# Moving two products of a gated linear recurrence from VectorE to GpSimd, and its decay constant into ScalarE's scale operand

## The chip, the core and the metric

The kernel runs on one core of one Trainium2 chip. A core has engines with queues of their own, each of which works strictly in order: TensorE (PE in the profile; its weight loads are PEld), VectorE (DVE), ScalarE (ACT), GpSimd (POOL) and SyncE (SP), which only issues transfers here. They wait for each other through semaphores. The metric is the device time of one execution in microseconds (us), lower is better; the times given are medians of several runs.

## The reference

The computation is three transformer-like layers for one sequence of 256 tokens with a width of 2048: a block of sparse attention and a mixture of 32 experts, an "even" layer and an "odd" layer. The change touches only the even layer. Its first half is a gated linear recurrence with 1024 channels in 8 blocks of 128:

```python
def rg_lru(x, gx_w, gx_b, ga_w, ga_b, lru_lambda):
    B, S, _ = x.shape
    xb = x.reshape(B, S, LRU_BLOCKS, LRU_BLOCK_DIM)
    gate_i = jax.nn.sigmoid(jnp.einsum("bsnd,nde->bsne", xb, gx_w) + gx_b).reshape(B, S, LRU_WIDTH)
    gate_r = jax.nn.sigmoid(jnp.einsum("bsnd,nde->bsne", xb, ga_w) + ga_b).reshape(B, S, LRU_WIDTH)
    log_a = -LRU_C * jax.nn.softplus(-lru_lambda.astype(jnp.float32)) * gate_r.astype(jnp.float32)
    a = jnp.exp(log_a)
    mult = jnp.sqrt(-jnp.expm1(2.0 * log_a))
    u = mult * gate_i.astype(jnp.float32) * x.astype(jnp.float32)
...
    _, h = lax.associative_scan(combine, (a, u), axis=1)
    return h.astype(x.dtype)
...
    y_a = rg_lru(lru_x, gx_w, gx_b, ga_w, ga_b, lru_lambda) * jax.nn.silu(lru_gate)
```

The second half is sliding-window attention. Both halves are joined and multiplied by the output weights `w_out`.

## The kernel before

Everything is stored with channels on the 128 partitions and the 256 tokens along the free axis. A projection is done in single chunks of 128 output channels. Its weights arrive as two halves of 128x1024; ScalarE rounds each half to a high part (`hi`, L1636), VectorE subtracts to get the low part (`lo`, L1945), and TensorE multiplies high by high, low by high and high by low (L1185): 24 matmuls of 128x256 for a half, 48 for a chunk. Four halves are kept in split form, so ScalarE and VectorE split a half while TensorE uses an earlier one.

The order of the work is written out by hand. `order_bc` makes one list of steps for each engine, and each engine runs its list from top to bottom, waiting before a step for the named steps of other engines. The stretch that matters here is the loop over the 24 chunks `bs`, `lx`, `lg` (window gate, recurrence input, recurrence gate; 8 of each). It mixes three kinds of work:

- The projections themselves. ScalarE moves a result out of PSUM (L1588 for `lx`, L1590 for `lg`), and GpSimd multiplies it by the row norm (`rms`, L2421, 128x256). Those products are all that GpSimd does in this stretch.
- Attention jobs, one after every second chunk. VectorE prepares the softmax (`soft`: L1865 mask, L1868 maximum, L1872 to L1874 small sums), ScalarE takes the exponentials (`exp`, L1722, L1724), VectorE divides (`scale`: L1882, L1883, L1898), TensorE transposes (`T`, L1119), ScalarE copies (`pt`, L1733), TensorE multiplies with the values (`O`, L1127), VectorE multiplies with the gate (`out`, L1911).
- The recurrence, in four pairs of blocks, started after chunks `lx 3`, `lx 6`, `lg 1` and `lg 4` (pairs 0 to 3). TensorE computes both gates (`lgate`, L1401); ScalarE takes sigmoids (L1600, L1601); VectorE multiplies the input gate by the input and the decay gate by its constant (`lruA`, L2294, L2295); ScalarE takes the exponential and the tangent of both blocks at once (`lruB`, L1747, L1748); VectorE combines them (`lruC`, L2300, L2301); ScalarE takes a root (`lruD`, L1751); VectorE multiplies and scans (`lruE`, L2307, L2308). `lruB` and `lruC` follow one chunk after the gates, `lruD` and `lruE` two chunks after.

After `lg 3` ScalarE applies silu to the first four gate chunks (L1684) and VectorE multiplies them with the first four blocks of the recurrence (`lmul 0`, L2312, 128x1024); `lmul 1` does the rest after `lg 7`. The result is then split for the output projection `wb` (L1671 and L1964).

The gates of the odd block of a pair go to one of the two PSUM banks of the projections. So the next but one projection that needs this bank waits for the sigmoids (L1601).

Of the kernel before, what the change touches and what calls it, by code (L numbers as in the profile page):

```python
# [19 lines left out]
ALU = mybir.AluOpType  # L20
# [23 lines left out]
LRU_C = 8.0  # L44
# [548 lines left out]
def order_bc():  # L593
# [53 lines left out]
    def lru_gates(p):  # L647
        for n in (2 * p, 2 * p + 1):
            o.add("pe", "lgate", n)
            if n % 2:  # L650
                o.acc.append(("lgate", n))
            o.add("act", "evac", ("lgate", n))
            o.add("dve", "lruA", n)
# [10 lines left out]
    for k, x in enumerate(rest):  # L664
# [12 lines left out]
        if x == ("lg", 3):  # L677
            o.add("act", "silu", "lg", 0, 4)
            o.add("dve", "lmul", 0)
# [119 lines left out]
def program(nc, t):  # L799
    with ExitStack() as ctx:  # L800
# [111 lines left out]
        cL, tsp = small[:, 144:152], small[:, 152:192]  # L912
# [586 lines left out]
        def _(act):  # L1499
# [8 lines left out]
            def run(k, o):  # L1508
# [5 lines left out]
                def needs(engine, *step):  # L1514
                    act.wait_ge(done[k][engine], o.at[engine][step])
# [99 lines left out]
                for step in o.steps["act"]:  # L1615
# [44 lines left out]
                    elif what == "mh":  # L1660
# [8 lines left out]
                        if made_by:  # L1669
                            needs("dve", *made_by)  # L1670
# [73 lines left out]
                    elif what == "lruB":  # L1744
                        p = step[1]
                        needs("dve", "lruA", 2 * p + 1)
                        act.activation(W(bLA, 2), W(bGR, 2), ACT.Exp, scale=-1.0)  # L1747
                        ins = act.activation(W(bTH, 2), W(bGR, 2), ACT.Tanh)  # L1748
# [50 lines left out]
        def _(dve):  # L1799
# [32 lines left out]
            def run(k, o):  # L1832
# [6 lines left out]
                def needs(engine, *step):  # L1839
                    dve.wait_ge(done[k][engine], o.at[engine][step])  # L1840
# [81 lines left out]
                for step in o.steps["dve"]:  # L1922
# [330 lines left out]
                    elif what == "softplus2":  # L2253
# [15 lines left out]
                        prod = W(aQI)[:, 0, 0:128].rearrange("p (a d) -> p a d", a=2)  # L2269
                        dve.tensor_scalar(cL, cL, LRU_C, None, ALU.mult)  # L2270
# [19 lines left out]
                    elif what == "lruA":  # L2290
                        n = step[1]
                        needs("act", "evac", ("lgate", n))
                        g = W(bGR + n % 2)[:, 0, :]
                        dve.tensor_tensor(W(bGI + n % 2)[:, 0, :], W(bGI + n % 2)[:, 0, :], W(bY + n)[:, 0, :], ALU.mult)  # L2294
                        ins = dve.tensor_scalar(g, g, cL[:, n:n + 1], None, ALU.mult)  # L2295
# [6 lines left out]
                    elif what == "lruE":  # L2302

                        n = step[1]
                        needs("act", "lruD", n // 2)
                        gi, th, a = (W(z + n % 2)[:, 0, :] for z in (bGI, bTH, bLA))
# [95 lines left out]
        def _(pool):  # L2402
# [3 lines left out]
            for count, (what, x) in enumerate(BC.steps["pool"]):  # L2406
                if count:
                    pool.wait_ge(done[1]["pool"], count)
                if what == "lo":
# [4 lines left out]
                                             WHs[1][:, x % PARTS, 0:n].bitcast(F32), ALU.subtract)  # L2414
                elif what == "rms":
# [122 lines left out]
```

## Time and profile before

| | us |
|---|---|
| median of 3 runs | 2349.46 |
| lowest, highest | 2347.33, 2351.78 |
| the profiled execution's own time | 2358.7 |
| its span, first to last instruction | 2356.9 |

| engine | busy us | share of the span |
|---|---|---|
| PE | 2089.4 | 89% |
| DVE | 1252.0 | 53% |
| ACT | 858.9 | 36% |
| POOL | 55.2 | 2% |

The shares are means over stages with different limits. Of the whole span only about 115 us, from 1615 to 1730 us after its start, hold the work that the change touches. A row of the timeline gives the start of an instruction, its length, its engine, its line, what it wrote and read, and in brackets how long its engine had been idle before it and which instruction ended that. A row of the windows gives a stretch, its length, the busy time of each engine in it (with the number of instructions), and PEclk, the granted clock of TensorE as a share of 2.4 GHz: 1.00 is 2.4 GHz and 0.50 is 1.2 GHz.

### The profile page before, as it was taken

What the parts mean: (1) busy time and instruction counts of PE and PEld (TensorE: products, weight loads), DVE (VectorE), ACT (ScalarE), POOL (GpSimd) and SP (SyncE); (2) the same over time, 40 slices, a digit from 0 to 9 for tenths busy, and PEclk for the clock granted to TensorE, in tenths of its full rate; (3) what the DMA queues carried; (4) which work ended last, traced back from release to release, by engine and by line L of the source; (5) the groups of instructions that cost most, each with busy time, mean ns of one, the idle gap of its engine ahead of it and who ended that gap; (6) DMA issues with size and microseconds to landing.
All of it is one profiled execution on the core that took longest, in us unless ns stands there. A gap on an engine that the chain in (4) does not pass through costs nothing.

```text
span 2356.9 us, 38440 instructions
## 1 busy us (share of the span) xinstructions
PE 2089.4 (89%) x14538; PEld 1364.2 (58%) x14538; DVE 1252.0 (53%) x2281; ACT 858.9 (36%) x1312; POOL 55.2 (2%) x56
## 2 busy tenths in 40 slices
PE   6899998989988888888888888999999999997997
PEld 2677766762222222222222222998889999997887
DVE  3455567545444444444444445558866454577655
ACT  3333344431111111111111113457855444565543
POOL 0000000000000000000000001011100010010000
PEclk9999999999999999999999999999999999998998
DMA  9998987899999999999999999463445455542442
GB/s 368 354 348 291 310 285 233 299 350 364 427 428 428 428 427 427 427 428 428 428 427 427 427 428 372 166 208 121 134 152 182 153 177 182 175 147 88 135 134 91
DMA packets 135047, 695.43 MB, mean 295 GB/s; under 512 B 14992, under 2 KB 15120, under 8 KB 85264
## 3 DMA queue, kind: packets, MB, share of 16 engines
q1 hardware_dynamic: 134928, 693.79, 76.7%
q8 instruction: 81, 1.33, 0.2%
q14 instruction: 38, 0.31, 0.0%
HBM read 691.63 MB, written 2.10 MB: 294 GB/s over the span
## 4 chain that ended last, share of the span: by engine, by line
PE 49%; DMA 34%; DVE 8%; ACT 4%; SPq 3%; issue 2%; DVEq 0%; ACTq 0%
PE acc L1185 34%; DMA ring<-in_w 30%; DMA land<-in_stream_a 3%; PE psO L1237 3%; PE psS L1468 3%; PE acc L1182 3%; DVE WL L1945 2%; SPq L1043 2%; ACT WH L1636 1%; DMA land<-in_stream_bc 1%; PE psM L1454 1%; PE acc L1454 1%; PE psT L1119 1%; ACT SB L1722 0%; PE psO L1127 0%
## 5 line engine op out<-in xcount | busy, mean ns | idle before, releaser
L1185 PE MATMUL acc<-HH,WH 128*128 128x256 f32 x2152 | 633.8, 295 | 11.8 <-DVE HL L1969 5.4
L1945 DVE TENSOR_TENSOR WL<-land,WH 128x1024 fp32r<-128x1024 f32 (+2 forms) x346 | 417.4, 1208 | 417.7 <-ACT WH L1636 413.6
L1185 PE MATMUL acc<-HH,WL 128*128 128x256 f32 x2152 | 616.0, 286 | 0.0
L1185 PE MATMUL acc<-HL,WH 128*128 128x256 f32 x2152 | 615.2, 286 | 0.0
L1636 ACT ACTIVATE WH<-land 128x1024 fp32r<-128x1024 f32 (+2 forms) x350 | 362.4, 1037 | 222.3 <-PE acc L1185 176.8
L1185 PEld LDWEIGHTS acc<-HH,WH 128*128 128x128 f32 x2152 | 420.5, 195 | 34.6 <-issue 11.6
L1185 PEld LDWEIGHTS acc<-HH,WL 128*128 128x128 f32 x2152 | 420.6, 195 | 2.0 <-issue 1.0
L1185 PEld LDWEIGHTS acc<-HL,WH 128*128 128x128 f32 x2152 | 419.9, 195 | 0.0
L1468 PE MATMUL psS<-ring,low 128*32 128x512 f32 x2048 | 273.9, 607 | 105.3 <-DMA ring<-in_w 100.8
L1468 PEld LDWEIGHTS psS<-ring,low 128*32 128x32 f32 x2048 | 40.8, 108 | 316.4 <-DMA ring<-in_w 285.0
L2355 DVE TENSOR_TENSOR X<-acc,X 128x512 f32<-128x512 f32 x128 | 88.6, 692 | 218.9 <-PE acc L1454 218.9
L1787 ACT ACT_TABLE_LOAD x32 | 41.1, 1283 | 447.1 <-PE psS L1468 447.1
L2355 DVE TENSOR_TENSOR X<-psM,X 128x512 f32<-128x512 f32 x128 | 88.6, 692 | 210.0 <-PE psM L1454 210.0
L1492 PE MATMUL psO<-ring,SB 128*32 128x512 f32 x1024 | 122.3, 598 | 42.9 <-DVE SB L2389 35.8
L1454 PE MATMUL psM<-low 128*128 128x512 f32 x264 | 150.4, 652 | 4.9 <-DVE low L2377 2.3
L1454 PE MATMUL acc<-low 128*128 128x512 f32 x264 | 149.3, 647 | 1.4 <-DVE X L2096 1.4
L1787 ACT ACTIVATE low<-psS 128x512 f32<-128x512 f32 x64 | 38.2, 597 | 244.6 <-PE psS L1468 244.2
L1237 PE MATMUL psO<-land,high_a 128*32 128x512 f32 x672 | 96.1, 648 | 35.2 <-DMA land<-in_stream_a 34.4
L1454 PEld LDWEIGHTS psM<-low 128*128 128x128 f32 x264 | 39.7, 189 | 116.6 <-DVE X L2355 80.5
L1454 PEld LDWEIGHTS acc<-low 128*128 128x128 f32 x264 | 39.5, 188 | 112.4 <-DVE X L2355 107.6
L1185 PE MATMUL acc<-lowR,WH 128*128 128x256 f32 x512 | 95.4, 289 | 5.8 <-DVE lowR L1964 5.8
L1492 PEld LDWEIGHTS psO<-ring,SB 128*32 128x32 f32 x1024 | 27.1, 109 | 116.6 <-DVE SB L2389 43.4
(370 smaller groups left out, 2413.4 us busy)
## 6 DMA issues: line engine op xcount, KB each, us to landing
ring<-in_w SPq DMA_DIRECT2D x384, 1024.0 KB, 26.0
land<-in_stream_a SPq DMA_DIRECT2D x284, 512.0 KB, 7.6
land<-in_stream_bc SPq DMA_DIRECT2D x246, 512.0 KB, 4.0
land<-in_stream_bc SPq DMA_DIRECT2D x12, 384.0 KB, 3.5
X<-in_xT SPq DMA_DIRECT2D x1, 2048.0 KB, 14.0
out<-low SPq DMA_DIRECT2D x4, 512.0 KB, 2.6
cst<-in_const SPq DMA_DIRECT2D x1, 1514.5 KB, 9.6
low<-in_w_pool SPq DMA_DIRECT2D x1, 1024.0 KB, 8.3
```

The costliest lines, as they stand in the source:

```text
L1043: sp.dma_start(ring[:, s, :], src[bass.ds(e, 1), s % 4, :, :].rearrange("e p n -> (e p) n")).then_inc(tile_in[s], 16)
L1119: mm = pe.transpose(psT[:, kt, h, :], SB[:, n % 2, h, P * kt:P * kt + P], ident)
L1182: mm = pe.matmul(bank[:, S * tt:S * tt + S], h[rows[kk]][:, P * tt:P * tt + P], w[:, kk, :], start=(z == 0 and i == 0 and tt == 0), stop=s ...
L1185: mm = pe.matmul(bank[:, 0:S], w[:, kk, :], h[rows[kk]], start=(z == 0 and i == 0), stop=stop)
L1237: mm = pe.matmul(bank[CAP * c:CAP * c + CAP, :], cB[:, 4 * q + c, :], w[c // 2][:, c % 2, :], start=(q == 0), stop=(q == 3), tile_position ...
L1454: return pe.matmul(ybank[m % 2], OE[:, P * c:P * c + P], SJ[:, 2 * half:2 * half + 2, :], start=True, stop=True)
L1468: mm = pe.matmul(bH[s // 4][CAP * c:CAP * c + CAP, :], XG[:, k % 4, k // 4, :], ring[:, s, 512 * c:512 * c + 512], start=(s % 4 == 0), sto ...
L1492: mm = pe.matmul(bW2[CAP * c:CAP * c + CAP, :], AT[:, s - 8, :], ring[:, s, 512 * c:512 * c + 512], start=(s == 8), stop=(s == 11), tile_p ...
L1636: ins = act.activation(wh, src, ACT.Copy)
L1787: act.activation(HS[:, b, :], bankS[b], ACT.Copy).then_inc(moe["h_copied"], 1)
L1945: ins = dve.tensor_tensor(wl, src, wh, ALU.subtract)
L2355: dve.tensor_tensor(moe_out(m), ybank[m % 2].rearrange("p (a s) -> p a s", a=2), moe_out(m), ALU.add)\
```

## The change

Three things move. The product of input gate and input (first line of `lruA`) goes from VectorE's list to GpSimd's, for each of the 8 blocks. The product with the decay constant (second line of `lruA`) is dropped; ScalarE's `lruB` applies the constant as its scale operand instead. Since this constant differs from block to block, the two instructions over 512 columns become four over 256, with `cL` and its new negated copy `ncL` as scales. And `lmul 0` goes to GpSimd's list. `lmul 1` stays on VectorE in the order, since only its first call is changed. `lruE` now also waits for GpSimd's product.

```diff
@@ lru_gates(p)
             o.add("act", "evac", ("lgate", n))
-            o.add("dve", "lruA", n)
+            o.add("pool", "lruA", n)
@@ after x == ("lg", 3)
             o.add("act", "silu", "lg", 0, 4)
-            o.add("dve", "lmul", 0)
+            o.add("pool", "lmul", 0)
@@ ScalarE
                     elif what == "lruB":
                         p = step[1]
-                        needs("dve", "lruA", 2 * p + 1)
-                        act.activation(W(bLA, 2), W(bGR, 2), ACT.Exp, scale=-1.0)
-                        ins = act.activation(W(bTH, 2), W(bGR, 2), ACT.Tanh)
+                        for n in (2 * p, 2 * p + 1):
+                            g = W(bGR + n % 2)[:, 0, :]
+                            act.activation(W(bLA + n % 2)[:, 0, :], g, ACT.Exp, scale=ncL[:, n:n + 1])
+                        for n in (2 * p, 2 * p + 1):
+                            g = W(bGR + n % 2)[:, 0, :]
+                            ins = act.activation(W(bTH + n % 2)[:, 0, :], g, ACT.Tanh, scale=cL[:, n:n + 1])
@@ VectorE
+                        dve.tensor_scalar(ncL, cL, -LRU_C, None, ALU.mult)
                         dve.tensor_scalar(cL, cL, LRU_C, None, ALU.mult)
...
-                    elif what == "lruA":
-                        n = step[1]
-                        needs("act", "evac", ("lgate", n))
-                        g = W(bGR + n % 2)[:, 0, :]
-                        dve.tensor_tensor(W(bGI + n % 2)[:, 0, :], W(bGI + n % 2)[:, 0, :], W(bY + n)[:, 0, :], ALU.mult)
-                        ins = dve.tensor_scalar(g, g, cL[:, n:n + 1], None, ALU.mult)
...
                         needs("act", "lruD", n // 2)
+                        needs("pool", "lruA", n)
@@ GpSimd
+                elif what == "lruA":
+                    needs("act", "evac", ("lgate", x))
+                    needs("dve", "conv", x)
+                    z = W(bGI + x % 2)[:, 0, :]
+                    ins = pool.tensor_tensor(z, z, W(bY + x)[:, 0, :], ALU.mult)
+                elif what == "lmul":
+                    needs("act", "silu", "lg", 4 * x, 4)
+                    needs("dve", "lruE", 4 * x + 3)
+                    z = W(MIX + 4 * x, 4)
+                    ins = pool.tensor_tensor(z, z, W(bY + 4 * x, 4), ALU.mult)
```

The names in the rows below: `low` and `high_bc` are the working tensors in SBUF, `psS` and `psO` are PSUM, `WL`, `WH` and `land` are a weight half's low part, high part and landing place, `SB` holds softmax rows, `small` holds columns.

VectorE around `lmul 0` before, from the last scan of pair 2 (L2308) on:

```order
L2308 SCALAR_TENSOR_TENSOR low<-high_bc 128x256
L1865 SCALAR_TENSOR_TENSOR SB<-psS,small,cst 128x1024
L1868 TENSOR_REDUCE small<-SB 128x4
L1872 TENSOR_TENSOR small<-small,col 128x4
L1873 TENSOR_TENSOR small<-col,small 128x4
L1874 TENSOR_SCALAR small<-small 128x4
L2312 TENSOR_TENSOR low<-low 128x1024
L1945 TENSOR_TENSOR WL_52<-land_58,WH_50 128x1024 x2
L2294 TENSOR_TENSOR high_bc<-high_bc,low 128x256
L2295 TENSOR_SCALAR high_bc<-high_bc,small 128x256
```

and now (lines are some numbers higher; L2307 is the scan, L1868 to L1877 the `soft` step, L1948 the weight split):

```order
L2307 SCALAR_TENSOR_TENSOR low<-high_bc 128x256
L1868 SCALAR_TENSOR_TENSOR SB<-psS,small,cst 128x1024
L1871 TENSOR_REDUCE small<-SB 128x4
L1875 TENSOR_TENSOR small<-small,col 128x4
L1876 TENSOR_TENSOR small<-col,small 128x4
L1877 TENSOR_SCALAR small<-small 128x4
L1948 TENSOR_TENSOR WL_52<-land_58,WH_50 128x1024 x4
```

The large product behind the softmax step and the four small ones of pair 3 are gone from VectorE; the four weight splits now stand in a row.

GpSimd's whole list before, from its last constant on:

```order
L2532 MEMSET const-uint8-127 128x1
L2401 UNCONDITIONAL_BRANCH
L2413 ISA
L2413 TENSOR_TENSOR WL_52<-land_58,WH_50 128x1024 x4
L2421 TENSOR_TENSOR low<-low,high_bc 128x256 x48
```

and now, from the three row norms of `lx 7`, `lg 0` and `lg 1` on (L2430 is `rms`, L2418 `lruA`, L2423 `lmul 0`):

```order
L2430 TENSOR_TENSOR low<-low,high_bc 128x256 x3
L2418 TENSOR_TENSOR high_bc<-high_bc,low 128x256 x2
L2430 TENSOR_TENSOR low<-low,high_bc 128x256 x2
L2423 TENSOR_TENSOR low<-low 128x1024
L2430 TENSOR_TENSOR low<-low,high_bc 128x256
L2418 TENSOR_TENSOR high_bc<-high_bc,low 128x256 x2
L2430 TENSOR_TENSOR low<-low,high_bc 128x256 x27
```

The large product stands between the row norms of `lg 3` and `lg 4`. On VectorE it stood behind the scans of pair 2 and the softmax step; on GpSimd it waits only for silu and for the scan of block 3, which is long done.

## Rows read from the trace of the kernel before

**Rows 1.** The page's first part: busy us (share of the span) and instructions by engine.

```profile
PE 2089.4 (89%) x14538; PEld 1364.2 (58%) x14538; DVE 1252.0 (53%) x2281; ACT 858.9 (36%) x1312; POOL 55.2 (2%) x56
```

**Rows 2.** Windows: stretch, length, busy time by engine, PEclk, DMA share, GB/s.

```profile
1636.30:1638.70 2.40, 0.05 (x2) 0.01 (x1) 2.25 (x9) 1.44 (x2) 0.72 (x1) 1.00 0.78 273
1638.70:1697.00 58.30, 58.30 (x420) 52.46 (x420) 53.32 (x95) 48.34 (x85) 5.74 (x6) 0.97 0.37 122
1697.00:1705.30 8.30, 6.37 (x50) 5.90 (x50) 6.44 (x15) 8.05 (x13) 1.35 (x1) 1.00 0.57 169
```

**Rows 3.** Timeline of PE: matmuls that started after an idle stretch.

```profile
1638.69 1.23 PE L1119 MATMUL psT<-cst,SB 128*128 128x128 f32 x8 [2.35 <-DVE SB L1898]
...
1698.63 0.39 PE L1185 MATMUL acc<-HH,WH 128*128 128x256 f32 x1 [1.35 <-ACT high_bc L1601]
...
1705.21 1.09 PE L1119 MATMUL psT<-cst,SB 128*128 128x128 f32 x8 [0.57 <-DVE SB L1898]
...
1717.24 0.36 PE L1185 MATMUL acc<-lowR,WH 128*128 128x256 f32 x1 [3.48 <-DVE lowR L1964]
...
1825.06 0.76 PE L1291 MATMUL psM<-high_bc,ones 128*128 128x256 f32 x1 [4.20 <-DVE high_bc L2109]
...
2232.89 0.36 PE L1185 MATMUL acc<-HH,WH 128*128 128x256 f32 x1 [1.86 <-DVE HL L1964]
```

**Rows 4.** Windows right behind such idle stretches, for PEclk.

```profile
1638.70:1643.00 4.30, 4.30 (x17) 3.64 (x17) 4.04 (x9) 1.02 (x1) 0.00 (x0) 0.60 0.19 72
1699.00:1703.00 4.00, 4.00 (x36) 4.00 (x35) 3.28 (x5) 3.91 (x5) 1.35 (x1) 1.00 0.34 93
1825.00:1831.00 6.00, 5.94 (x27) 5.79 (x28) 0.72 (x2) 0.42 (x1) 0.00 (x0) 0.53 0.35 124
2233.00:2237.00 4.00, 4.00 (x22) 4.00 (x23) 3.62 (x4) 0.00 (x0) 0.00 (x0) 0.57 0.30 112
```

**Rows 5.** Timeline of ACT, from `lruB` of pair 2 to the sigmoids of pair 3.

```profile
1678.76 0.63 ACT L1747 ACTIVATE high_bc<-high_bc 128x512 f32<-128x512 f32 x1
1679.30 0.61 ACT L1748 ACTIVATE high_bc<-high_bc 128x512 f32<-128x512 f32 x1
...
1685.76 1.06 ACT L1684 ACTIVATE low<-low 128x1024 f32<-128x1024 f32 x1
...
1692.09 1.28 ACT L1722 ACT_TABLE_LOAD   x1 [1.38 <-DVE small L1874]
...
1696.87 0.47 ACT L1600 ACTIVATE high_bc<-psM,col 128x256 f32<-128x256 f32 x1
1697.24 0.47 ACT L1601 ACTIVATE high_bc<-psM,col 128x256 f32<-128x256 f32 x1
```

**Rows 6.** Timeline of DVE in the same stretch.

```profile
1680.02 0.69 DVE L2300 TENSOR_TENSOR high_bc<-high_bc 128x512 f32<-128x512 f32 x1 [1.20 <-ACT high_bc L1748]
...
1687.08 0.69 DVE L2308 TENSOR_TENSOR_SCAN low<-high_bc 128x256 f32<-128x256 f32 x1
...
1692.04 1.23 DVE L2312 TENSOR_TENSOR low<-low 128x1024 f32<-128x1024 f32 x1
```

**Rows 7.** One line's instructions each: shortest/median/longest in ns, first and last start.

```profile
L2294 DVE TENSOR_TENSOR high_bc<-high_bc,low x8: 424/426/898, 1623.5 to 1698.7; 128x256 f32<-128x256 f32 x8
L2295 DVE TENSOR_SCALAR high_bc<-high_bc,small x8: 342/348/348, 1624.3 to 1699.0; 128x256 f32<-128x256 f32 x8
L1958 DVE SCALAR_TENSOR_TENSOR HL<-X,col,HH x32: 484/485/1733, 1461.8 to 1818.0; 128x256 fp32r<-128x256 f32 x32
```

**Rows 8.** Timeline of POOL: four large products, two small ones.

```profile
1457.47 9.79 POOL L2413 TENSOR_TENSOR WL<-land,WH 128x1024 fp32r<-128x1024 f32 x4 [1457.04 <-ACT WH L1636]
...
1623.34 0.75 POOL L2421 TENSOR_TENSOR low<-low,high_bc 128x256 f32<-128x256 f32 x1 [9.51 <-ACT low L1588]
...
1689.15 0.73 POOL L2421 TENSOR_TENSOR low<-low,high_bc 128x256 f32<-128x256 f32 x1 [5.86 <-ACT low L1590]
```

**Rows 9.** Timeline of DVE under the large products of GpSimd.

```profile
1463.32 1.73 DVE L1958 SCALAR_TENSOR_TENSOR HL<-X,col,HH 128x256 fp32r<-128x256 f32 x1
```

More of the change, by code:

```diff
@@ L911, in program @@
         jst = small[:, 112:144].rearrange("p (b k h) -> p b k h", b=2, k=4)
-        cL, tsp = small[:, 144:152], small[:, 152:192]
+        cL, tsp, ncL = small[:, 144:152], small[:, 152:192], small[:, 160:168]
         wis = small[:, 208:240]
@@ L1669, in run @@
                         if made_by:
-                            needs("dve", *made_by)
+                            needs("pool" if made_by == ("lmul", 0) else "dve", *made_by)
                         ins = act.activation(mix_split(k, name, 4 * c, 4)[0], W(MIX + 4 * c, 4), ACT.Copy)
```

## The prediction

> **What bounds the kernel now.** I read the page first. TensorE is busy for 89% of the span, VectorE for 53%, GpSimd for 2% [rows 1]. A VectorE that is half idle is no bottleneck over the whole, so taking work from it pays only where TensorE waits for it. The second view is therefore the timeline of TensorE over the stretch of the recurrence, looked through for idle time. Three waits lie in it before the output projection: 2.35 us for the `scale` step of an attention job (wait A), 1.35 us for the sigmoids of pair 3 (wait B) and 0.57 us for another `scale` step (wait C) [rows 3]. Between A and B TensorE is busy for 58.30 of 58.30 us although VectorE is busy for 53.32 of them [rows 2]: there VectorE is nearly full and still not late. The 3.48 us in front of the output projection [rows 3] hang on the last projection's move out of PSUM and on the attention's output, which the change leaves alone, and `lmul 1` stays where it was. So all that can be won or lost sits in A, B and C, 4.27 us in sum, and in the clock behind them.
>
> The clock is the third view. Behind wait A the mean clock was 0.60 for 4.30 us; behind a wait of 1.86 us late in the span it was 0.57 for 4.00 us; behind one of 4.20 us it was 0.53 for 6.00 us; behind wait B, 1.35 us, it stayed at 1.00 [rows 3, 4]. 0.50 is 1.2 GHz. What a fall costs is length times missing clock: 4.30 x 0.40 = 1.7 us behind A, 4.00 x 0.43 = 1.7 us behind the wait of 1.86 us, 6.00 x 0.47 = 2.8 us behind the one of 4.20 us. A wait that grows from 1.35 us to beyond 1.86 us pays this on top.
>
> **The change, part by part.**
>
> *The decay constant.* It removes 8 VectorE instructions of 0.348 us [rows 7], 2.8 us in all. None of it is on the path. VectorE's `lruC` starts when ScalarE has ended `lruB`: before it VectorE sat idle for 1.20 us in pair 2 [rows 6], and the same holds in pair 0, where the chain that ends wait A runs. VectorE's gain turns into a longer idle time there. ScalarE pays: the two instructions over 512 columns take from 1678.76 to 1679.30 + 0.61 = 1679.91, 1.15 us [rows 5]. Four over 256 columns are not in this trace with these functions; the nearest are the sigmoids, which start 0.37 us apart [rows 5], so four take 4 x 0.37 + 0.10 for the tail of the last = 1.58 us, 0.43 us more (bounds: 0.2 us, if a source in SBUF makes each cheaper by 0.05, and 0.7 us, if they do not overlap and take 0.47 each). I take 0.43. In pairs 1 and 3 it is hidden behind ScalarE's later wait for a projection. In pair 0 ScalarE's end of `lruB` starts the VectorE chain up to `scale`, so wait A becomes 0.43 longer. In pair 2 it starts the chain up to wait B, 0.43 again. Everything behind A moves by the first, everything behind B by both.
>
> *The gate product.* It takes 8 instructions of 0.426 us from VectorE [rows 7] and puts 8 of 0.75 us on GpSimd [rows 8], which has the time. But the engines are not independent. The longest L2294 took 0.898 in place of 0.426 us [rows 7]: it started at 1623.5, in the middle of a GpSimd product of 0.75 us from 1623.34 [rows 8]. So a GpSimd product of 256 columns holds back a VectorE instruction with two SBUF operands by 0.47 us, a little more than VectorE saves by giving the product away. For pairs 1 and 2 VectorE loses up to 2 x 0.47 = 0.9 us and gains 2 x (0.43 + 0.35) = 1.6 us, in a stretch where TensorE has no idle time. In pairs 0 and 3 the products fall where VectorE works from PSUM or waits for ScalarE. I put the part at 0; bounds -0.3 and +0.5 us, if one of them falls into a chain that ends in A or C. The queue matters as well: GpSimd works in order, and behind these products wait the row norms, which the convolution and the silu need. Before two of them GpSimd was idle for 9.51 and 5.86 us [rows 8], so there is room for 1.5 us.
>
> *The output gating, `lmul 0`.* This is the term that decides. On VectorE it takes 1.23 us at 1692.04 [rows 6], behind the `soft` step for which ScalarE waits, so it delays nobody; removing it gains nothing. On GpSimd it becomes ready when silu ends, 1685.76 + 1.06 = 1686.82, plus the 0.43 of pair 2 = 1687.25 in the frame of before [rows 5]. At this time VectorE is in `lruE` of pair 2: product, scan, product, scan, all with two SBUF operands. The first scan starts at 1687.08 [rows 6], moved by 0.43 to 1687.51, so `lmul 0` gets in right before it. Behind the four stands `soft`, then ScalarE's exponentials (which waited 1.38 us for it [rows 5]), the sigmoids and wait B. VectorE has no slack in this chain.
>
> How long does a product of 1024 columns hold VectorE? The four large GpSimd products took 9.79 us, 2.45 each [rows 8]. A product of 256 columns takes 0.75 and holds 0.47, so the large one holds about 0.47 + (2.45 - 0.75) = 2.17 us. A lower bound is in the trace: under them an instruction of 0.485 us took 1.73 [rows 7, 9], held for 1.25 us at least, since it came in the middle. An upper bound is 2.45. I take 2.17, on the rows' own scaling.
>
> Then the row norm of `lg 4`, which ran at 1689.15 under a VectorE step that reads PSUM and cost nothing [rows 8], stands behind `lmul 0` on GpSimd. It now starts near 1689.9, still between the delayed scans, and holds VectorE for another 0.47 (lower bound 0, if it comes after the last scan).
>
> The Trainium skill (SBUF — State Buffer, "Who interferes with whom") says that GpSimd and VectorE share one pair of ports as an exclusive lock for the whole instruction, and that only VectorE instructions with two SBUF inputs or in a two-port mode are concerned. The second half agrees with the rows. The first half says more than they do: 0.47 us of 0.75 were lost.
>
> *Wait B and its clock.* B grows by 0.43 + 2.17 + 0.47 = 3.07 us, from 1.35 to 4.42 us. At that length the clock falls, and the projection behind it loses between 1.7 and 2.8 us, 2.3 taken. This slower projection uses up wait C, which the chain over ScalarE and VectorE sets: 0.57 us come back. Net 1.7 (bounds 1.1 and 2.3).
>
> *The rest.* One more instruction on 8 columns in the set-up (`ncL`), and one more semaphore wait in `lruE`, long fulfilled: under 0.1 us, beside the first transfers.
>
> The sum: 0.43 (A) + 3.07 (B) + 1.7 (clock less C) = 5.2 us. The profiled execution took 2358.7 us, so 2363.9 by its measure. It lies 9.2 us above the median of the runs shown, which has to do with the execution and not with the change; the same 5.2 us on 2349.46 give **2354.7 us**, 0.22% more. A measurement of this kernel can tell about 0.2% (4.7 us) from no change.
>
> **The rivals.**
>
> *GpSimd is the one that waits.* If `lmul 0` gets its operands only when VectorE leaves them, that is from the `soft` step on (which reads PSUM), the chain is not held. Against it: the L2294 of 0.898 us. For it: the trace of before has no GpSimd product of 1024 columns beside a scan. Then A and B each grow by 0.43; B is 1.78 us, between the 1.35 that left the clock alone and the 1.86 that did not. 2350.3 us without the fall, 2350.3 + 1.7 - 0.57 = 2351.5 us with it.
>
> *VectorE is held for the whole of each GpSimd instruction.* The place is the same, the price 2.45 + 0.75 = 3.20 in place of 2.64 us, and B reaches 4.98 us with the long fall of the clock, 2.8 - 0.57 = 2.3: 0.43 + 3.63 + 2.3 = 6.3, 2355.8 us. It decides as soon as the hold is over 2.3 us. This is the rule of the skill's page taken word for word.
>
> *VectorE's relief counts.* In pair 0 VectorE is rid of four instructions, 1.5 us, before the chain of wait A. If that chain began when VectorE is free and not when `lruB` ends, A would vanish with its clock: 2.35 + 1.7 = 4.0 us, 2345.4 us. Against it: VectorE was idle before `lruC` in that chain, and ScalarE's end only moves later.
>
> **How the numbers follow.** Forecast 0.62, GpSimd waits 0.19, whole instruction 0.14, relief 0.05. The likeliest gives 2354.7, its own range from its bounds 2352.0 to 2357.0. For 8 in 10 the range has to take in most of the second case and the scatter of the runs (2347.33 to 2351.78 for one kernel): 2349.5 to 2358. The forecast lies 0.5 us above the limit of 0.2%, so it splits about 0.37 slower, 0.24 same, 0.01 faster; the second case is nearly all same (0.19), the third 0.12 slower and 0.02 same, the last 0.01 same and 0.04 faster. In sum: faster 0.05, same 0.46, slower 0.49.
>
> **What the profile after would show.** VectorE's scans of pair 2: one near 2.9 us in place of 0.69, beside the 128x1024 product of GpSimd. TensorE's wait before the projection behind the sigmoids of pair 3: 4.4 us in place of 1.35, and PEclk near 0.5 behind it. The wait for `scale` behind it gone. Wait A near 2.8 us; `lruB` near 1.6 us. It would be wrong if GpSimd's large product is long and the scans are not, if silu ends before or after the scans, or if four short activations cost as much as two long ones.

## The result and the profile after

| | before | after |
|---|---|---|
| median of 17 runs each, us | 2347.1 | 2353.09 |
| lowest, highest, us | 2342.55, 2351.78 | 2348.05, 2365.65 |
| span of the profiled execution, us | 2356.9 | 2354.7 |

The ratio is 1.0029 with an interval of 1.0019 to 1.0040: the changed kernel is slower by 6.8 us (4.5 to 9.4) by this ratio, a little more than the 5.2 us forecast; the two medians lie 6.0 us apart. The two profiled executions end in the other order. TensorE's mean granted clock late in the program differs between them, 0.94 before and 0.96 after from 2100 to 2340 us, far behind the changed stretch, so the spans can't be compared. What can be compared in one execution is the stretch that the change touches, from the first gate matmul of pair 0 (L1401) to the waits in front of the output projection.

The timeline of PE after; the first row is that matmul, the others started after an idle stretch. A is the second row, B the third; the fourth and fifth are the two waits of the output projection, called D and E from here on (D is the 3.48 us of [rows 3]).

```profile
1612.56 1.13 PE L1401 MATMUL psM<-low 128*128 128x256 f32 x4
...
1636.76 1.42 PE L1119 MATMUL psT<-cst,SB 128*128 128x128 f32 x8 [2.83 <-DVE SB L1901]
...
1699.72 0.58 PE L1185 MATMUL acc<-HH,WH 128*128 128x256 f32 x1 [4.47 <-ACT high_bc L1601]
...
1720.54 0.55 PE L1185 MATMUL acc<-lowR,WH 128*128 128x256 f32 x1 [3.88 <-DVE lowR L1967]
...
1732.74 0.43 PE L1185 MATMUL acc<-lowR,WH 128*128 128x256 f32 x1 [2.36 <-DVE lowR L1967]
```

And before, the start of the same stretch and its end E (A, B, C and D stand in [rows 3]):

```profile
1614.96 1.13 PE L1401 MATMUL psM<-low 128*128 128x256 f32 x4
...
1728.49 0.58 PE L1185 MATMUL acc<-lowR,WH 128*128 128x256 f32 x1 [2.37 <-DVE lowR L1964]
```

A grew from 2.35 to 2.83, B from 1.35 to 4.47, D from 3.48 to 3.88 us, and C (0.57) is gone. From the first gate matmul to D it was 1717.24 - 1614.96 = 102.28 us before and 1720.54 - 1612.56 = 107.98 us after, 5.70 more. Of these the waits are 0.48 + 3.12 - 0.57 + 0.40 = 3.43 us. The other 2.27 us are TensorE's own work at a lower clock, as the windows behind B show (columns as in [rows 2]; [rows 4] has 1.00 behind B before):

```profile
1699.70:1701.70 2.00, 1.98 (x9) 1.98 (x10) 0.84 (x1) 1.94 (x3) 1.09 (x2) 0.50 0.01 4
1701.70:1703.70 2.00, 2.00 (x11) 2.00 (x11) 1.72 (x2) 1.97 (x3) 0.97 (x1) 0.50 0.30 47
1703.70:1705.70 2.00, 2.00 (x12) 2.00 (x11) 1.85 (x8) 1.97 (x5) 0.00 (x0) 0.51 0.85 258
1705.70:1708.00 2.30, 2.30 (x21) 2.30 (x21) 2.20 (x6) 0.68 (x1) 0.00 (x0) 1.00 0.58 192
```

The cause of B is on VectorE, in `lruE` of pair 2 and the `soft` step behind it. It answers to [rows 6], where the scan took 0.69 us:

```profile
1685.70 2.81 DVE L2307 TENSOR_TENSOR_SCAN low<-high_bc 128x256 f32<-128x256 f32 x1
1688.54 0.78 DVE L2306 TENSOR_TENSOR high_bc<-high_bc 128x256 f32<-128x256 f32 x1
1689.36 0.69 DVE L2307 TENSOR_TENSOR_SCAN low<-high_bc 128x256 f32<-128x256 f32 x1
1690.09 1.28 DVE L1868 SCALAR_TENSOR_TENSOR SB<-psS,small,cst 128x1024 f32<-128x1024 f32 x1
```

Beside it on GpSimd, `lmul 0` and then the row norm of `lg 4` (columns the same):

```profile
1685.58 2.38 POOL L2423 TENSOR_TENSOR low<-low 128x1024 f32<-128x1024 f32 x1 [3.67 <-issue]
1688.04 1.00 POOL L2430 TENSOR_TENSOR low<-low,high_bc 128x256 f32<-128x256 f32 x1
```

The scan was held for 2.81 - 0.69 = 2.12 us by the first, the product behind it for 0.78 - 0.43 = 0.35 us by the second; the last scan has its 0.69 us again. ScalarE then waited 4.50 us for `soft` (1.38 in [rows 5]), 3.12 us more, and B grew by the same 3.12 us.

ScalarE's `lruB` of pair 2, to be read against the first two of [rows 5]:

```profile
1676.83 0.91 ACT L1748 ACTIVATE high_bc<-high_bc,small 128x256 f32<-128x256 f32 x2
1677.64 0.89 ACT L1751 ACTIVATE high_bc<-high_bc,small 128x256 f32<-128x256 f32 x2
```

From the first start to the last end it is 1677.64 + 0.89 - 1676.83 = 1.70 us, against 1.15 before.

### The profile page after: what moved, and what is told of

Read it like the earlier page. It is cut to its first block, busy times and chain, and to the rows that moved or that the text cites. A ratio compares the mean times of both kernels' runs of the same rounds, so it can differ in the third digit from the quotient of the medians.

```text
span 2354.7 us, 38437 instructions
## 1 busy us (share of the span) xinstructions
PE 2086.2 (89%) x14538; PEld 1360.7 (58%) x14538; DVE 1248.8 (53%) x2265; ACT 861.2 (37%) x1320; POOL 64.6 (3%) x65
## 4 chain that ended last, share of the span: by engine, by line
PE 49%; DMA 34%; DVE 8%; ACT 4%; SPq 3%; issue 2%; DVEq 0%; ACTq 0%
PE acc L1185 33%; DMA ring<-in_w 30%; DMA land<-in_stream_a 3%; PE psO L1237 3%; PE psS L1468 3%; PE acc L1182 3%; DVE WL L1948 2%; SPq L1043 2%; ACT WH L1636 1%; DMA land<-in_stream_bc 1%; PE psM L1454 1%; PE acc L1454 1%; ACT SB L1722 1%; PE psM L1237 1%; PE psO L1127 0%
## 5 line engine op out<-in xcount | busy, mean ns | idle before, releaser
L1948 DVE TENSOR_TENSOR WL<-land,WH 128x1024 fp32r<-128x1024 f32 (+2 forms) x346 | 418.1, 1210 | 418.3 <-ACT WH L1636 414.3
```

The costliest lines, as they stand in the source:

```text
L1948: ins = dve.tensor_tensor(wl, src, wh, ALU.subtract)
```

## The experiments

For each kernel the table gives the ratio to the kernel before with its interval, the difference of the stretch from the first gate matmul to D and to E (before: 102.28 and 113.53 us), the difference of all waits above 0.15 us in the stretch to D, D among them, and what is left, nearly all of it the clock's (shorter gaps make 0.13 us of it in e6 and e10, 0.28 us in e9 and e11, and nothing elsewhere). The differences of time come from one execution each.

| kernel | ratio | to D | to E | waits to D | rest |
|---|---|---|---|---|---|
| after | 1.0029 [1.0019, 1.0040] | +5.70 | +6.65 | +3.43 | +2.27 |
| e1 without `lmul 0` | 1.0005 [0.9993, 1.0016] | +1.95 | +2.63 | +0.99 | +0.96 |
| e2 only `lmul 0` | 1.0025 [1.0011, 1.0039] | +3.58 | +3.57 | +2.31 | +1.27 |
| e3 only the constant | 1.0020 [1.0006, 1.0034] | +2.17 | +3.16 | +1.00 | +1.17 |
| e4 only the gate product | 0.9993 [0.9978, 1.0008] | +0.02 | +0.01 | -0.11 | +0.13 |
| e5 `lmul 0` one place later | 1.0006 [0.9995, 1.0016] | +2.23 | +2.25 | +1.23 | +1.00 |
| e8 `lmul 0` in quarters | 1.0002 [0.9988, 1.0015] | +3.29 | +3.28 | +2.22 | +1.07 |
| e6 before, all pairs later | 1.0022 [1.0009, 1.0035] | +1.15 | +2.27 | +2.51 | -1.36 |
| e7 e1, all pairs later | 1.0013 [0.9999, 1.0028] | +1.01 | +2.00 | +2.55 | -1.54 |
| e9 order in two places | 0.9993 [0.9979, 1.0007] | -2.30 | -2.27 | -1.35 | -0.95 |
| e10 e9 and e4 | 0.9989 [0.9975, 1.0002] | -0.63 | -0.64 | -0.97 | +0.34 |
| e11 order, pair 0 alone | 1.0008 [0.9992, 1.0023] | -1.50 | -0.38 | -0.53 | -0.97 |
| e12 order, pair 2 alone | 1.0003 [0.9988, 1.0018] | -1.34 | -1.36 | -1.35 | +0.01 |

0.001 is 2.35 us, so an interval is some 3.5 us to each side. The difference of the stretch to E lies inside the ratio's interval for all thirteen kernels, though nine of the intervals hold 1 as well, so this is a weak check. The waits resolve what the medians don't: those of the three parts alone, 2.31 + 1.00 - 0.11 = 3.20 us, nearly add up to the 3.43 of the whole change. The whole stretch adds up better still, 3.57 + 3.16 + 0.01 = 6.74 us to E against 6.65 (to D 3.58 + 2.17 + 0.02 = 5.77 against 5.70), but that is in part chance. e2 and e3 each have a slow clock behind B, the whole change has one only, and a longer one: over the 6 us behind B the clock was 0.72 in e2 and in e3, and 0.51 in the changed kernel.

How long the slow clock lasts differs even behind equal waits, and this moves the stretch by about 1 us. Behind D, 3.48 us in both, the 7 us ran at 0.76 in the kernel before and at 0.58 in e11, in this order:

```profile
1717.24:1724.24 7.00, 7.00 (x46) 7.00 (x47) 4.71 (x4) 4.26 (x4) 0.00 (x0) 0.76 0.13 49
```

```profile
1711.17:1718.17 7.00, 7.00 (x37) 7.00 (x38) 3.85 (x4) 4.26 (x4) 0.00 (x0) 0.58 0.13 50
```

All thirteen changed kernels and the one before follow this: where these 7 us ran at 0.76 (before, e2, e4, e5, e8, e9, e10, e12) the way from D to E took 11.23 to 11.27 us, and where they ran at 0.57 to 0.64 (after, e1, e3, e6, e7, e11) 11.94 to 12.37 us. The length of D doesn't decide it: at 3.88 to 3.91 us both kinds occur (0.60 after, 0.76 in e5).

### e1: the change without the move of `lmul 0`

```diff
-            o.add("pool", "lmul", 0)
+            o.add("dve", "lmul", 0)
...
```

> The changed kernel with one part undone: the large product of 128x1024 (lmul 0) is VectorE's again. Theory (GpSimd's large product holds VectorE's scans): the two scans of pair 2 are back at 0.69 us, the wait in front of the projection behind the sigmoids of pair 3 (4.47 us in the changed kernel) falls to 1.35 + 0.56 = 1.9 us, the wait for the scale step before pair 1's gates stays at 2.83 us, and the time is 0.5 to 1.5 us above the kernel before (ratio 1.0002 to 1.0006) if the clock stays up behind the wait of 1.9 us, up to 1.1 us more if it falls. Rival (the loss comes from ScalarE's four short activations and the small products on GpSimd): the ratio stays near 1.0029 and the wait stays over 4 us.

The waits were 2.83 (A), 2.02 (B), 3.89 (D) and 2.36 us (E), C was gone, and the scans were back at 0.69 us. So B without the hold is 2.02 us, and the move of `lmul 0` makes the other 4.47 - 2.02 = 2.45 us of it (2.12 + 0.35 = 2.47 us of hold). Yet the clock had fallen behind B here too, over 4 us with 0.60:

```profile
1700.18:1704.18 4.00, 4.00 (x21) 4.00 (x22) 2.58 (x2) 3.91 (x5) 2.08 (x2) 0.60 0.40 128
```

### e2: the kernel before with `lmul 0` on GpSimd and nothing else

```diff
-            o.add("dve", "lmul", 0)
+            o.add("pool", "lmul", 0)
...
```

> The kernel before with one part done alone: only lmul 0 goes to GpSimd. Theory: one scan of pair 2 takes 2.8 us and the product behind it 0.8 us, the wait in front of the projection grows from 1.35 by 2.5 to 3.8 us, the clock falls behind it, the wait for the scale step before pair 1 stays at 2.35 us; time 2.5 + 1.1 to 2.5 + 2.3 = 3.6 to 4.8 us above before, ratio 1.0015 to 1.0021. Rival (the loss is in the other two parts): ratio 1.0000, wait 1.4 us.

The mechanism doesn't need the other two parts. DVE and POOL in this kernel:

```profile
1684.22 2.81 DVE L2308 TENSOR_TENSOR_SCAN low<-high_bc 128x256 f32<-128x256 f32 x1
1687.06 0.78 DVE L2307 TENSOR_TENSOR high_bc<-high_bc 128x256 f32<-128x256 f32 x1
```

```profile
1684.09 2.39 POOL L2419 TENSOR_TENSOR low<-low 128x1024 f32<-128x1024 f32 x1 [3.66 <-issue]
1686.56 0.99 POOL L2426 TENSOR_TENSOR low<-low,high_bc 128x256 f32<-128x256 f32 x1
```

A stayed 2.35, B became 3.80 (+2.45), C vanished, D became 3.91 us.

### e3: the kernel before with the constant in the scale operand and nothing else

```diff
-                        act.activation(W(bLA, 2), W(bGR, 2), ACT.Exp, scale=-1.0)
-                        ins = act.activation(W(bTH, 2), W(bGR, 2), ACT.Tanh)
+                        for n in (2 * p, 2 * p + 1):
+                            g = W(bGR + n % 2)[:, 0, :]
+                            act.activation(W(bLA + n % 2)[:, 0, :], g, ACT.Exp, scale=ncL[:, n:n + 1])
+                        for n in (2 * p, 2 * p + 1):
+                            g = W(bGR + n % 2)[:, 0, :]
+                            ins = act.activation(W(bTH + n % 2)[:, 0, :], g, ACT.Tanh, scale=cL[:, n:n + 1])
...
-                        ins = dve.tensor_scalar(g, g, cL[:, n:n + 1], None, ALU.mult)
```

> The kernel before with one part done alone: the decay constant goes into the scale operand (four activations over 256 columns in place of two over 512, eight multiplications gone from VectorE), both products stay on VectorE. Theory: lruB takes 1.74 in place of 1.18 us, the wait for the scale step grows from 2.35 to 2.8 us, the one behind the sigmoids of pair 3 from 1.35 to 1.9 us, time +1.0 us (ratio 1.0004), or +2.1 us if the clock falls behind the second. Rival (VectorE's relief of 2.8 us counts): both waits shorter, ratio under 1.

The ratio came out above the 1.0004 to 1.0009 expected, with an interval that reaches down to 1.0006: A 2.83 and B 2.02 us as in e1, D 3.90, and a clock that fell behind B. So 8 instructions less on VectorE came with 2.2 us more in the stretch to D (3.2 to E, where 1.0 is the longer slow clock behind D): an instruction was taken from an engine that waits at this point and put on one that is waited for. That e1, with the same waits, has a ratio lower by 0.0015 is within what the intervals leave.

### e4: the kernel before with the gate product on GpSimd and nothing else

```diff
+            o.add("pool", "lruA", n)
...
-                        dve.tensor_tensor(W(bGI + n % 2)[:, 0, :], W(bGI + n % 2)[:, 0, :], W(bY + n)[:, 0, :], ALU.mult)
...
```

> The kernel before with one part done alone: the eight gate products of 128x256 go to GpSimd, the decay constant stays a VectorE multiplication, lmul 0 stays on VectorE. Theory: VectorE gives away 8 x 0.43 us and loses up to 0.47 us for each product that meets one of its instructions with two SBUF operands; no chain that ends in a wait of TensorE changes, waits 2.35 and 1.35 us, ratio 1.0000 within 0.0005. Rival (small GpSimd products on the critical chain cost too): a wait grows by 0.4 us or more, ratio 1.0003 or above.

Neutral within 0.02 us of the stretch. One new wait of 0.31 us for a `scale` step appeared in pair 2's place, and B fell from 1.35 to 0.92 us:

```profile
1666.62 1.09 PE L1120 MATMUL psT<-cst,SB 128*128 128x128 f32 x8 [0.31 <-DVE SB L1899]
...
1691.89 0.39 PE L1186 MATMUL acc<-HH,WH 128*128 128x256 f32 x1 [0.92 <-ACT high_bc L1602]
```

The new wait is a hold. The first instruction of this `scale` step (DVE), over 4 columns and 0.16 us long before, started under GpSimd's two gate products of pair 2 (POOL):

```profile
1664.65 0.52 DVE L1883 TENSOR_TENSOR small<-small 128x4 f32<-128x4 f32 x1
```

```profile
1663.45 1.69 POOL L2420 TENSOR_TENSOR high_bc<-high_bc,low 128x256 f32<-128x256 f32 x2 [2.07 <-ACT high_bc L1602]
```

B is shorter because TensorE reached it 0.45 us later, not because the sigmoids came earlier: B ended 83.68 us after the first gate matmul, and 83.67 us in the kernel before. So small gate products can hold the chain too, and here the next wait took the loss up.

### e5: the changed kernel with `lmul 0` one place later in GpSimd's list

`lmul 0` stands behind the row norm of `lg 4` in place of in front of it.

```diff
+        if x == ("lg", 4):
+            o.add("pool", "lmul", 0)
...
-            o.add("pool", "lmul", 0)
```

> The changed kernel with lmul 0 still on GpSimd, but one place later in its list, behind the row norm of lg 4. Theory (only VectorE instructions with two SBUF operands are held): the large product now starts about 0.6 us after the last scan of pair 2, under the softmax step, whose mask reads PSUM and whose maximum has one operand; they keep their 1.28 and 1.22 us, only the tiny step behind them may wait 0.2 us. The wait in front of the projection is 2.0 to 2.3 us in place of 4.47; ratio to before 1.0005 to 1.0015, like the kernel with lmul 0 back on VectorE. Rival (a GpSimd product of 1024 columns holds whatever VectorE runs): wait over 4 us, ratio 1.003.

VectorE, then GpSimd:

```profile
1680.41 0.69 DVE L2308 TENSOR_TENSOR_SCAN low<-high_bc 128x256 f32<-128x256 f32 x1
1681.14 1.28 DVE L1869 SCALAR_TENSOR_TENSOR SB<-psS,small,cst 128x1024 f32<-128x1024 f32 x1
1682.46 1.22 DVE L1872 TENSOR_REDUCE small<-SB 128x4 f32<-128x1024 f32 x1
1683.71 0.42 DVE L1876 TENSOR_TENSOR small<-small,col 128x4 f32<-128x4 f32 x1
```

```profile
1681.71 2.40 POOL L2424 TENSOR_TENSOR low<-low 128x1024 f32<-128x1024 f32 x1
```

The same product, 2.40 us long, now lies under an instruction that reads PSUM and a reduction, and neither is longer than before. Only the sum over 4 columns (0.16 us otherwise) was caught by its end, for 0.26 us. B was 2.27 us in place of 4.47, for one place in a list. The stretch to D was 3.5 us shorter than after, 2.2 us of it in the waits (to E 4.4 us); the rest is the clock, whose slow time behind B and behind D was shorter here.

### e8: the changed kernel with `lmul 0` as four products of 128x256

```diff
-                    z = W(MIX + 4 * x, 4)
-                    ins = pool.tensor_tensor(z, z, W(bY + 4 * x, 4), ALU.mult)
+                    for q in range(4):
+                        z = W(MIX + 4 * x + q)[:, 0, :]
+                        ins = pool.tensor_tensor(z, z, W(bY + 4 * x + q)[:, 0, :], ALU.mult)
```

> The changed kernel with lmul 0 on GpSimd as four products of 128x256 in place of one of 128x1024. Theory (the hold lasts for one GpSimd instruction and VectorE gets its turn between two): product, scan, product and scan of pair 2 are held by 0.4 us each at most, 1.2 to 1.6 us in all in place of 2.5; the wait in front of the projection is 3.1 to 3.6 us in place of 4.47, the clock still falls; ratio to before 1.0020 to 1.0027. Rival (the hold is by total work): the four together hold VectorE for 2 us or more, wait 4.4 us.

```profile
1682.15 1.17 DVE L2307 TENSOR_TENSOR_SCAN low<-high_bc 128x256 f32<-128x256 f32 x1
1683.36 0.77 DVE L2306 TENSOR_TENSOR high_bc<-high_bc 128x256 f32<-128x256 f32 x1
1684.17 1.10 DVE L2307 TENSOR_TENSOR_SCAN low<-high_bc 128x256 f32<-128x256 f32 x1
```

Held for 0.48, 0.34 and 0.41 us, 1.23 us in sum, beside GpSimd instructions that take 3.77 us together. Between two of them VectorE gets in; B was 3.25 us, 1.22 less than after. The ratio, 1.0002, came out below the expected 1.0020 to 1.0027, while the stretch to E (+3.28 us, 1.0014) is inside its interval.

### e6 and e7: the recurrence one chunk later in every pair

e6 is the kernel before, e7 the kernel e1, each with

```diff
-            o.lagged.append((1, lru_decay, p))
-            o.lagged.append((2, lru_scan, p))
+            o.lagged.append((2, lru_decay, p))
+            o.lagged.append((3, lru_scan, p))
```

> The kernel before with lruB and lruC of each pair one chunk later, and lruD and lruE one more, nothing on GpSimd. Theory (both waits are ended by VectorE chains in which lruC, and for the second one lruE too, stand before the step that is waited for): the wait for the scale step of 2.35 us shrinks by 1.4 us or more and no longer pulls the clock down, the wait of 1.35 us behind the sigmoids of pair 3 goes; ratio 0.998 to 0.999 (3 to 5 us less). Rival (the steps only change places and delay the next ones): new waits of the same sum before the output projection, ratio 1.000 or more.

> The same delay of the decay steps, on the changed kernel with lmul 0 back on VectorE (gate product on GpSimd, constant in the scale operand). Theory: with the recurrence off the chains in front of the two waits, ScalarE's 0.56 us more for each pair is hidden and VectorE's relief neither helps nor harms; ratio within 0.0005 of the other kernel with later decay steps. Rival (the relief of VectorE counts once the order is better): 0.0005 or more below it.

A vanished and others came. In e6 D is 5.85 in place of 3.48 us, since pair 3's scans now stand in front of the split for the output projection, and small waits appeared where pairs 1 and 2 have moved to:

```profile
1651.37 0.66 PE L1119 MATMUL psT<-cst,SB 128*128 128x128 f32 x4 [0.68 <-DVE SB L1898]
...
1668.18 1.09 PE L1119 MATMUL psT<-cst,SB 128*128 128x128 f32 x8 [1.22 <-DVE SB L1898]
...
1694.48 0.39 PE L1185 MATMUL acc<-HH,WH 128*128 128x256 f32 x1 [1.94 <-ACT high_bc L1601]
...
1715.48 0.55 PE L1185 MATMUL acc<-lowR,WH 128*128 128x256 f32 x1 [5.85 <-DVE lowR L1964]
```

Both are misses: e6 was expected below 1, and e7 within 0.0005 of e6. e7's ratio is lower by 0.0009, which was the rival's sign that VectorE's relief counts, but the two intervals overlap over most of their length, and its stretch is only 0.1 us shorter to D and 0.3 us to E. Its waits show no help from the relief (D 5.84, B 1.93 us).

### e9 to e12: the order in one or two places

e9 is the kernel before with pair 0 one chunk later and pair 2's root and scan directly behind the `soft` step at `lg 3`; e10 adds the gate product on GpSimd, e11 is pair 0 alone, e12 pair 2 alone.

```diff
-            o.lagged.append((1, lru_decay, p))
-            o.lagged.append((2, lru_scan, p))
+            o.lagged.append((2 if p == 0 else 1, lru_decay, p))
+            if p != 2:
+                o.lagged.append((3 if p == 0 else 2, lru_scan, p))
         if x == ("lg", 3):
+            lru_scan(2)
```

> The kernel before with the order changed in two places: the exponential/tangent step and the combining step of pair 0 stand one chunk later, its root, product and scan too; in pair 2 the root, product and scan stand directly behind the softmax step of the job before, in front of silu. Theory (both waits are ends of chains of which the recurrence steps are a movable part): wait A goes from 2.35 us to below 0.3 us and its clock stays at 1.00; wait B goes from 1.35 us to below 0.5 us; the 3.48 us and 2.37 us in front of the output projection stay. Saved: 2.35 + 1.7 + 1 = 4 to 5 us, ratio 0.998. Rival (as in the delay of all pairs, steps only change places and meet others): new waits of 2 us or more in sum in the stretch, ratio 1.000 or more.

> The same order, with the product of gate and input on GpSimd as well. Theory (this part is about neutral alone, since its GpSimd instructions last 0.75 us and meet few of VectorE's products): the waits of the kernel with the order alone, each within 0.5 us, ratio the same or up to 0.0007 lower. Rival (VectorE held in the place where it now has no reserve): a wait of TensorE longer by 0.5 us or more than with the order alone, and a ratio higher by 0.0005 or more.

> The kernel before with the order changed for pair 0 alone. Theory (wait A costs its length and the slow clock behind it, and nothing later gives it back): wait A below 0.3 us, B 1.35, D 3.48 and E 2.37 us as before, PEclk 1.00 behind the place of A; ratio 1 - 4.0 / 2348 = 0.9983. Rival (TensorE only arrives earlier at a later wait): B, D or a wait between A and B grows by what A lost, ratio 0.9995 to 1.0005.

> The kernel before with the order changed for pair 2 alone: its root, product and scan stand directly behind the softmax step of the job before, in front of silu. Theory (of the two moves only this one saves time, since the other only displaced wait A): wait A stays 2.35 us with its slow clock, wait B falls from 1.35 us to below 0.3 us, the waits in front of the output projection stay 3.48 and 2.37 us; from the first gate matmul of pair 0 to the second wait of the output projection 1.3 to 1.9 us less than in the kernel before (113.53 us), ratio 0.9992 to 0.9994. Rival (the move for pair 0 was needed, since the relief of B in the joint kernel came from the chain that starts earlier): B stays above 1 us, the stretch within 0.3 us of the kernel before.

TensorE's waits in e9; there is none left at B:

```profile
1651.83 0.66 PE L1121 MATMUL psT<-cst,SB 128*128 128x128 f32 x4 [0.68 <-DVE SB L1900]
...
1669.49 0.77 PE L1121 MATMUL psT<-cst,SB 128*128 128x128 f32 x5 [1.67 <-DVE SB L1900]
...
1700.42 1.09 PE L1121 MATMUL psT<-cst,SB 128*128 128x128 f32 x8 [0.57 <-DVE SB L1900]
...
1712.47 0.55 PE L1187 MATMUL acc<-lowR,WH 128*128 128x256 f32 x1 [3.48 <-DVE lowR L1966]
```

Pair 2's move takes B away whole (e12: B gone, the others 2.35, 0.57 and 3.48 us, stretch -1.34 to D). Pair 0's move is the rival come true in length: A's 2.35 us stand again as 0.69 + 1.66 us at the next two attention jobs (e11), 0.68 + 1.67 in e9. Part of the second is a hold by GpSimd. The four products of the `scale` step, in front of this wait, take 1.14 us in e4, and here, with the row norm of a projection beside them, 1.62 us (e11, DVE and then POOL):

```profile
1665.71 1.62 DVE L1898 TENSOR_SCALAR SB<-SB,small 128x256 f32<-128x256 f32 x4
```

```profile
1666.37 0.81 POOL L2421 TENSOR_TENSOR low<-low,high_bc 128x256 f32<-128x256 f32 x1 [5.52 <-ACT low L1590]
```

Only B gave way in e11, from 1.35 to 0.82 us. What the move saves is the slow clock behind A, since the clock stayed at 1.00 behind both new waits; that is worth 0.95 to 0.97 us (1.23 to 1.25 if the gaps below 0.15 us count as waits). It hardly shows at E in e11 (-0.38 us), because of the longer slow clock behind D, which e9 doesn't have.

In e10 GpSimd's pair of gate products (2.43 us for two, where each alone takes 0.74) lies beside two weight splits of VectorE, which take 2.96 in place of 2.48 us; the wait there is 2.13 in place of 1.67 us, and the clock falls behind it:

```profile
1664.82 2.96 DVE L1948 TENSOR_TENSOR WL<-land,WH 128x1024 fp32r<-128x1024 f32 x2
```

```profile
1670.80:1674.80 4.00, 4.00 (x21) 4.00 (x22) 3.75 (x9) 2.45 (x3) 0.00 (x0) 0.57 0.07 26
```

By the stretch e10 is 1.6 us worse than e9, by the ratios 0.0004 better; the intervals (0.9975 to 1.0002, and 0.9979 to 1.0007) don't tell them apart. Neither is shown to beat the kernel before, though both lie below it; against the changed kernel, e9 is better: their intervals don't meet.

## Why the prediction was right

The predicted 2354.7 us was 5.2 us above the median it started from; measured were 6.8 us (4.5 to 9.4). Point by point:

- **A, +0.43.** Measured +0.48. The cause is the one named: e3, which has only the scale operand, has the same 2.83 us.
- **Four activations for two, +0.43.** Measured 1.70 against 1.15 us, +0.55. The sigmoids start 0.37 us apart [rows 5], these (1677.64 - 1676.83) / 2 = 0.405. The Trainium skill (ScalarE: Activation LUTs, "What ACT_TABLE_LOAD costs") gives 186 ns plus 0.833 ns per element, 93 ns more for each operand that is a column, and an overlap of 93 ns; worked out from it, 0.40 us apart and 0.56 us more for the four, an estimate that these rows agree with. B got 0.67 us longer by it (e1, e3), A 0.48; why B's share is 0.12 us above the 0.55 was not looked into.
- **The hold by `lmul 0`, +2.17, and by the row norm, +0.47.** Measured 2.12 and 0.35. B came to 4.47 us against 4.42. So close a match is in part luck, since two errors cancel: `lruB` added 0.24 us more than forecast (0.67 for 0.43), the hold 0.19 us less (2.45 for 2.64). That the mechanism is this and no other is shown by e2 (the hold alone, +2.45), e1 (without it, -2.45), and e5 (the same product under other instructions, -2.20).
- **The clock behind B, 2.3, less C, 0.57.** The rest to D is 2.27 us, and C is gone. The size was right, but by luck: in e2, with the same hold and a B of 3.80 us, the slow clock was shorter and the rest 1.27, in e8 (3.25 us) 1.07, in e5 (2.27 us) 1.00. Since such lengths differ behind equal waits too, as shown for D, about 1 us of the 2.27 is not shown to come from the length of B. The step's condition was wrong. It set the fall between 1.35 and 1.86 us of waiting, and so charged it to the hold. In e1 and e3 the clock falls at 2.02 us without any hold. The clock's cost thus belongs to the scale operand as much as to the hold: either brings the fall alone, with a rest of 1.17 us in e3 and 1.27 in e2.
- **A fall as length times missing clock.** This step was mis-sized. It gave 1.7 us for A; taking A away saved 0.95 to 1.25 us (e9, e11). For B in the changed kernel it would give 6 x 0.5 = 3.0 us where 2.27 remain. Behind A part of the slow time is transposes, which felt the clock little: eight took 1.23 us in [rows 3] behind A and 1.09 behind C.
- **D untouched.** Wrong, by 0.40 us. VectorE reaches the end of the chunks late, its last two weight splits stand together under GpSimd's row norm of `lg 7` (1.58 us), and take 2.89 us where two in a row take 2.48 without a GpSimd product beside them:

```profile
1715.35 2.89 DVE L1948 TENSOR_TENSOR WL<-land,WH 128x1024 fp32r<-128x1024 f32 x2
```

```profile
1715.59 1.58 POOL L2430 TENSOR_TENSOR low<-low,high_bc 128x256 f32<-128x256 f32 x1 [5.88 <-ACT low L1590]
```

  All kernels with the clock fallen behind B (after, e1, e2, e3, e5, e8) have D at 3.88 to 3.91; e4, e9 to e12, where it stood, have 3.48. Neither moved product is needed for it: e3 has both on VectorE and D at 3.90.
- **The small gate products at 0.** e4: 0.02 us in the stretch, inside the bounds, though one of them did fall into a chain, for 0.36 us.
- **The rivals.** GpSimd didn't wait: `lmul 0` began 0.13 us after silu's end, before the scan. VectorE's relief brought nothing that could be seen (e3, e7). The rule that VectorE is held for the whole GpSimd instruction was set aside with a wrong reading: the prediction took "0.47 of 0.75 us lost" as speaking against it. The VectorE instruction had started 0.16 us after GpSimd's. The next section has the numbers; read so, the rule gives the measured 2.47 us, and the rival's 3.20 was too much because VectorE's instructions started 0.12 and 0.50 us after GpSimd's.

The excess of the measured 6.8 us over the forecast, 1.6 us, is smaller than its interval. The 0.40 us of D are in it; the 0.95 us by which the way from D to E was longer after (12.20 against 11.25 us) go with the longer slow clock behind D, which e11 has behind an unchanged D and e5 has not behind the longer one, so they are not shown to come from the change.

## What to carry to other kernels

Before giving a product to an idle GpSimd, look up what VectorE does at the time when its operands become ready: beside instructions with two operands in SBUF it holds VectorE until it is nearly done, and a `tensor_scalar` with a single SBUF tensor was held too (0.48 us in e11); beside one that reads PSUM or a reduction it cost nothing, and one place in the queue decides which (2.2 us of waiting here). An instruction taken from VectorE is worth nothing at a point where VectorE waits for ScalarE, and if ScalarE pays for it, it is a loss. A wait on a chain that is moved as a whole tends to stand again at the next place; in one execution the waits between two fixed instructions resolve such changes far better than the median of a kernel that scatters by 10 us and more. The time between the two instructions is less sure than the waits: equal waits were followed by slow clocks of different length, and that alone moved it by 1 us.

## What the runs showed of the hardware

**The hold, in numbers.** For VectorE instructions with two operands in SBUF it is the time from VectorE's start to the end of the GpSimd instruction, less 0.14 us, in each of these cases: for the scan 1685.58 + 2.38 - 1685.70 - 0.14 = 2.12 (measured 2.12); for the product behind it 1688.04 + 1.00 - 1688.54 - 0.14 = 0.36 (0.35); for the sum over 4 columns in e5 1681.71 + 2.40 - 1683.71 - 0.14 = 0.26 (0.26); for the first instruction of `scale` in e4 1663.45 + 1.69 - 1664.65 - 0.14 = 0.35 (0.36); for the product of 0.898 us before, from the starts in [rows 7, 8], 0.45 (0.47). An instruction over 4 columns is held like a large one. The Trainium skill (SBUF — State Buffer, "Who interferes with whom") says that the engine that comes second is blocked until the first has finished; these rows agree.

GpSimd is delayed too: the row norm behind `lmul 0` took 1.00 us beside the tail of the scan, where it takes 0.74 alone.

**The clock.** Up to and with D it fell behind all waits of 2.02 us and more (0.50 to 0.68 over the next 4 us); behind 0.92, 1.35, 1.67, 1.80 (e7), 1.93 (e7) and 1.94 us (e6) it stayed at 1.00. But behind the 1.86 us of [rows 3] it fell, and behind E, 2.35 to 2.37 us long everywhere, it was 0.60 in the kernel before and 1.00 in e4, e9 and e10. So the length of the wait alone doesn't decide; what else does was not tested. The windows behind the 1.93 us of e7 and behind E in e4:

```profile
1691.68:1695.68 4.00, 4.00 (x33) 4.00 (x34) 2.58 (x2) 3.26 (x4) 2.09 (x2) 1.00 0.18 25
```

```profile
1721.75:1725.75 4.00, 4.00 (x33) 4.00 (x34) 0.42 (x1) 1.56 (x3) 0.00 (x0) 1.00 0.36 127
```
